# Sums of squares for the q and k norms as two rounded parts, with the gated-DeltaNet stages moved one or two k-tiles on

## The reference

```python
def l2norm(x):
    return x * lax.rsqrt(jnp.sum(x * x, axis=-1, keepdims=True) + EPS)
...
qkv, new_buf = causal_conv(jnp.concatenate([qg, kg, vg], axis=-1), conv_buf, conv_w)
q = l2norm(qkv[..., :GDN_KEY_W].reshape(B, L, GDN_HEADS, GDN_HEAD_DIM)) * (GDN_HEAD_DIM ** -0.5)
k = l2norm(qkv[..., GDN_KEY_W:2 * GDN_KEY_W].reshape(B, L, GDN_HEADS, GDN_HEAD_DIM))
v = qkv[..., 2 * GDN_KEY_W:].reshape(B, L, GDN_HEADS, GDN_HEAD_DIM)
```

## Time and profile before

| what | value |
| --- | --- |
| median of 3 runs | 3050.93 us (3047.31 to 3050.95) |
| the profiled execution's own time | 3054.05 us |
| its span, first to last instruction | 3052.3 us |
| PE busy | 2964.2 us, 22024 matmul records |
| DVE busy | 2036.2 us |
| ACT busy | 1203.9 us |
| POOL busy | 324.9 us |
| mean granted clock of TensorE | 0.990 of full speed |

### The profile page before, as it was taken

One profiled execution on the slowest core, in us unless ns is written; L12 is line 12 of the kernel. 1 busy time (PEld: TensorE's weight loads), 2 busy tenths in 40 slices (PEclk: granted clock), 3 DMA queues, 4 the chain that ended last, 5 costly groups with the idle time before them and its releaser, 6 DMA issues.

```text
span 3052.3 us, 52510 instructions
## 1 busy us (share of the span) xinstructions
PE 2964.2 (97%) x22024; PEld 2910.8 (95%) x22024; DVE 2036.2 (67%) x2828; ACT 1203.9 (39%) x1522; POOL 324.9 (11%) x433
## 2 busy tenths in 40 slices
PE   7999999999999999989999999999998999999998
PEld 7999999999999999988989999999997999999998
DVE  5556473747474656564567777777778878888885
ACT  4333333323333333332344444444444444444454
POOL 5010102011101010101210000000000000000111
PEclk9999999999999999999999999999999999999999
DMA  7233554523232334244334544445457666666665
GB/s 212 57 82 64 76 66 57 85 58 91 52 80 64 82 61 82 61 142 123 115 95 141 156 140 146 157 137 160 143 170 254 194 194 193 194 191 198 186 201 186
DMA packets 514107, 392.61 MB, mean 129 GB/s; under 512 B 16752, under 2 KB 483904, under 8 KB 513872
## 3 DMA queue, kind: packets, MB, share of 16 engines
q1 hardware_dynamic: 462272, 268.86, 35.9%
q0 software_dynamic: 22832, 88.39, 7.9%
q10 hardware_dynamic: 28768, 32.00, 3.6%
HBM read 304.87 MB, written 84.33 MB: 128 GB/s over the span
## 4 chain that ended last, share of the span: by engine, by line
PE 88%; DVE 7%; ACT 2%; issue 2%; DMA 1%; POOL 0%; DVEq 0%; SPq 0%; POOLq 0%; ACTq 0%
PE main L1268 39%; PE main L921 30%; PE mx L1268 6%; PE mx L1164 2%; PE mx L997 1%; PE mx L1065 1%; PE mx L1073 1%; PE mx L981 1%; DVE w_lo L1806 1%; DVE tmp L1914 1%; PE mx L1107 1%; ACT w_hi L1356 0%; PE mx L1171 0%; PE mx L1101 0%; PE mx L1045 0%
## 5 line engine op out<-in xcount | busy, mean ns | idle before, releaser
L921 PE MATMUL main<-h_hi,w_hi 128*128 128x296 f32 (+1 forms) x2592 | 612.1, 317 | 15.1 <-DVE h_lo L2164 8.4
L1268 PE MATMUL main<-forms_a,w_hi 128*128 128x288 f32 x3072 | 618.0, 297 | 8.7 <-DVE forms_a L2395 4.7
L1268 PE MATMUL main<-forms_b,w_hi 128*128 128x288 f32 x3072 | 613.9, 295 | 8.8 <-DVE forms_b L2395 5.0
L921 PE MATMUL main<-h_lo,w_hi 128*128 128x296 f32 (+1 forms) x2592 | 566.5, 300 | 0.0
L921 PE MATMUL main<-h_hi,w_lo 128*128 128x296 f32 (+1 forms) x2592 | 565.9, 300 | 0.0
L1268 PEld LDWEIGHTS main<-forms_a,w_hi 128*128 128x128 f32 x3072 | 497.1, 189 | 9.5 <-issue 9.3
L1268 PEld LDWEIGHTS main<-forms_b,w_hi 128*128 128x128 f32 x3072 | 492.1, 188 | 10.1 <-issue 5.6
L1268 PE MATMUL main<-forms_a,w_lo 128*128 128x288 f32 x1536 | 456.3, 297 | 0.0
L1268 PE MATMUL main<-forms_b,w_lo 128*128 128x288 f32 x1536 | 452.2, 294 | 0.0
L921 PEld LDWEIGHTS main<-h_hi,w_hi 128*128 128x128 f32 x2592 | 416.3, 191 | 27.2 <-DVE h_lo L2164 8.6
L921 PEld LDWEIGHTS main<-h_lo,w_hi 128*128 128x128 f32 x2592 | 423.7, 190 | 0.0
(11 more groups left out here) (383 smaller groups left out, 3685.0 us busy)
## 6 DMA issues: line engine op xcount, KB each, us to landing
w_raw<-in_w_in SPq DMA_DIRECT2D x130, 512.0 KB, 8.2
w_raw<-in_w_up SPq DMA_DIRECT2D x128, 512.0 KB, 4.1
w_raw<-in_w_down SPq DMA_DIRECT2D x100, 512.0 KB, 4.5
u_forms<-ub POOLq DMA_DIRECT2D x32, 1152.0 KB, 6.8
z<-x_scratch SPq DMA_DIRECT2D x32, 576.0 KB, 7.5
x_scratch<-z POOLq DMA_DIRECT2D x31, 576.0 KB, 3.1
stage<-u_forms ACTq DMA_DIRECT2D x30, 576.0 KB, 4.0
w_raw<-in_w_out SPq DMA_DIRECT2D x32, 512.0 KB, 4.0
```

What stands on the lines that cost most here:

```text
L921: ins = mm(out[:, half, :], w[:, ring, k, :], x[:, kx, half * width:half * width + width], start=first and n == 0, stop=last_ and n == 2)
L1268: ins = mm(out, w[:, k, :], x[:, kx, :], start=i in (0, 1, 3) and k == 0 and n == 0, stop=k == KP - 1 and n == 2, skip_group_check=True)
```

## The change

The squares are split as the projections' operands are. ACT writes a rounded copy `sq_hi` of the squares, DVE the rest `sq_lo` (in place of the squares), and PE multiplies both by a matrix of ones in `fp32r`: eight matmuls of one record each for four of two. Four GDN stages move by one or two positions, and all that come after them, but the last, by one: `norms` 14 to 16, `rows` 15 to 17, `scores` 20 to 21, `turn_v` 21 to 22, `turn_k` 22 to 23, `ws0` 23 to 24, `turn_r0` 24 to 25; the 32 stages from `t1` on filled 25 to 57 with one position free, and now fill 26 to 57 with none.

```diff
-GDN_STAGES = {"gates": 0, "norms": 14, "rows": 15, "scores": 20, "turn_v": 21, "turn_k": 22, "ws0": 23, "turn_r0": 24,
+GDN_STAGES = {"gates": 0, "norms": 16, "rows": 17, "scores": 21, "turn_v": 22, "turn_k": 23, "ws0": 24, "turn_r0": 25,
               **spread(["t1"] + T_STEPS + ["p64", "tp64", "vn0", "st0"]
-                       + [f"{s}_{c}" for c in range(1, NW) for s in ("ws", "vn", "st")], 25, 57),
+                       + [f"{s}_{c}" for c in range(1, NW) for s in ("ws", "vn", "st")], 26, 57),
...
+        sq_hi, sq_lo = (sq_mem[:, o:o + 2 * N].rearrange("p (a b) -> p a b", a=2) for o in (2 * 3 * CW + 5 * N, 2 * 3 * CW + 3 * N))
...
-                    token_sums(0, rs[:, 0, :])
-                    gpe.done(token_sums(2, rs[:, 1, :]), "norms")
+                    W(gdve, "sq_lo")
+                    for i in range(2):
+                        for half in range(2):
+                            cols = slice(half * HALF, half * HALF + HALF)
+                            mm(mx[:, 2 * i + half, 0:HALF], ones_r[:, :], sq_hi[:, i, cols], start=True, stop=False)
+                            ins = mm(mx[:, 2 * i + half, 0:HALF], ones_r[:, :], sq_lo[:, i, cols], start=False, stop=True)
+                    gpe.done(ins, "norms")
...
+                A(ones_r[:, :], ones[:, :], ACT.Copy)
...
                     done(A(rs, qkv[:, 0:2, :], ACT.Square), "square")
+                    W(gact, "square")
+                    done(A(sq_hi, rs, ACT.Copy), "sq_hi")
...
                 elif stage == "norms":
+                    W(gact, "sq_hi")
+                    done(TT(sq_lo, rs, sq_hi.bitcast(F32), ALU.subtract), "sq_lo")
                     W(gact, "rexp")
```

More of the change, by code:

```diff
@@ L197 @@
           + ["out"])
-GDN_ACT = (["conv_out", "exp", "ln", "sig", "zexp", "zln", "zsig", "square", "rln", "rexp", "brow", "eb", "decay",
+GDN_ACT = (["conv_out", "exp", "ln", "sig", "zexp", "zln", "zsig", "square", "sq_hi", "rln", "rexp", "brow", "eb", "decay",
             "vt", "r0", "t1"] + [f"{s}{b}" for b in INV[:-1] for s in ("p", "t")] + ["p64", "vn0", "o0"]
            + [f"{s}_{c}" for c in range(1, NW) for s in ("vn", "o")] + ["osq", "oln", "oexp"])
-GDN_DVE = (["conv_in", "conv_0", "conv_1", "conv_2", "last", "sel", "clamp", "zclamp", "qkv", "zs", "qn", "kn", "kb",
+GDN_DVE = (["conv_in", "conv_0", "conv_1", "conv_2", "last", "sel", "clamp", "zclamp", "qkv", "zs", "sq_lo", "qn", "kn", "kb",
             "vb", "diff", "keb", "qe", "dm", "at", "qkd", "tt0", "tt1", "kd", "r0"] + [f"t{b}" for b in INV[:-1]]
@@ L265, in hymba_kernel @@
         with ExitStack() as s:
+            sq_mem = sb("sq_mem", [P, 12200], F32R, stack=s)
+        with ExitStack() as s:
             tmp = sb("tmp", [P, 12200], stack=s)
@@ L290, in hymba_kernel @@
             one_hot = sb("one_hot", [16, 16], stack=s)
+            ones_r = sb("ones_r", [P, P], F32R, stack=s)
             dt_bias = sb("dt_bias_c", [16, 1], stack=s)
```

## The result

| | before | with the change |
| --- | --- | --- |
| median | 3049.67 us (3047.31 to 3050.95, 4 runs) | 3118.85 us (3113.84 to 3122.85, 4 runs) |
| ratio | | 1.0227, 95% interval 1.0215 to 1.0239 |
| span of the profiled execution | 3052.3 us | 3121.1 us |
| mean granted clock | 0.990 | 0.975 |

The change makes the kernel 69 us slower. The prediction said 3090, with a range of 3073 to 3106: the direction was right, the loss was 1.8 times the forecast of 39.

What follows compares the result with a forecast made beforehand. PE's nearly pauseless instruction list (busy 97%) was taken as the bound. Order 33.0, matmul saving included, plus clock 6 made 39 on the profiled 3054.05, or 3093; that execution lying 3.1 above the median, 3090 us, range 3073 to 3106.

Steps and rivals of the forecast that it cites:

- The order of the instructions: ACT's and DVE's order makes PE wait in each head: 4.13 us lost per head, 33.0 over eight, matmul saving included.
- the first stall: PE idles ahead of slot 10's first main matmul, waiting for DVE's weights: 2.66 us a head.
- the second: PE idles ahead of the norms, waiting for DVE's `sq_lo` behind an evacuation and a block of weights: 2.30 us a head.
- the move's own share: Part of the wait for slot 10's weights that the moved stages cause without the rounded copy: 1.43 us of 2.66.
- The third term: PE's wait ahead of the rows, for ACT's logarithm: 1.00 us a head in place of 0.78.
- The matmuls: Norms: eight `fp32r` records of 0.136, 1.09 us, replace eight of 0.235: 0.78 saved per head, 6.3 over eight.
- The stages behind: Stages after the rows (scores, `ws0`, slot 14) don't wait anew: together nothing, give or take 2 us.
- The clock: Every head loses full clock at least once; one half-speed stretch felt per head, 8 x 1.5 = 12, 6 more than now.
- The third rival: The clock stays down: two half-clock stretches per head fall on work, 33 + 18 = 51, 3102 us; chance 0.18.
- Only the matmuls count: ACT and DVE have both parts and slot 10's weights ready: gain 6.3, 3045, or 3039 if clock holds; chance 0.03.
- One stall only: Wait for slot 10's weights is real, but `sq_lo` is ready before PE reaches the norms: 3066 us; chance 0.08.
- the format does nothing: The norms' `fp32r` sums cost what the plain ones do: 33 + 6.3 + 6 = 45, 3096 us; chance 0.05.

Runs made afterwards that it cites:

- filled and padded kernel: Changed kernel with unread matmuls in place of PE's two stalls and the rows' matmuls on 128 partitions in place of 16: 3077.24 us, ratio 1.0097.
- padded kernel: Changed kernel with the rows' matmuls on 128 partitions, all but 16 holding zeros, in place of 16; both stalls stay: 3092.26 us, ratio 1.0140.
- rearranged program: Changed kernel with slot 10's weights made before the square, square, copy and rest before gate z is finished, rows at 18: 3037.93 us, ratio 0.9966.

## Why the prediction was wrong

**The order of the instructions: right.** By starts the first stall is 2.78 for 2.66, the second 2.29 for 2.30, the move's own share 1.54 for 1.43, with both releasers as named. The third term, a wait of 1.00 ahead of the rows in the place of 0.78, was not: in the filled and padded kernel it is 0.79 by starts, and in the changed kernel 0.15. The filled and padded kernel puts the price of the order at 32 us (4.0 a head) for the forecast 33.0.

**The matmuls: right.** Eight records in 1.15 us at full clock, for 1.09. In the changed kernel itself nothing of it arrives, as the norms run at half speed in 2.11.

**The stages behind: nearly right.** I had 2 us either way. A wait of 0.53 is new in each head: one of PE's transpositions in the inverse stands behind DVE's step `t32`, which now comes after slot 13's weights.

```profile
344.57 0.66 PE L1002 MATMUL mx<-ident,tmp 128*128 128x128 f32 x4 [0.54 <-DVE tmp L1997]
```

The prediction looked at the boundaries of slots 11 and 14 and not at this one. The wait of 0.91 of the earlier trace rows fell to 0.53 in exchange. That leaves 0.15 a head, about 1 us in all, inside the 2 us allowed.

**The clock: the step that failed.** The prediction says: "If one such stretch falls on work that PE can't hide in a stall, it is 8 x 1.5 = 12, 6 more than now; if two, 18 more; none at all, 6 less. I take 6, because slow k-tiles between two stalls only shorten the stalls." It took one short fall in each head as felt, 12 us in all less the 6 that the kernel before already pays. Measured is 44 us (5.5 a head) less the 5 that the kernel before pays (four falls of 1.3), so 39 in the place of 6. With 32 for the order that makes 71, beside 69 measured. The price of a stretch was about right, their number was not: four stretches end to end in every head, 4 x 1.5 = 6.0 by the prediction's own price, for 5.5 measured. The third rival, "the clock stays down", named the mechanism but stopped at two stretches, 3102, and so the range ended at 3106.

Two things were overlooked. The prediction expected slow k-tiles between the two stalls, where they would only shorten the second one. But the k-tile there ran at full speed; the clock fell at 294.4, late in the second stall, and took the norms, the k-tile behind, the rows and about three more k-tiles, which PE can't hide, so ACT's logarithm, too, started late. And the rows were counted at their length of full clock, though the kernel before shows that a wait of 0.61 and rows of 2.15 are enough to lose the clock in four of eight heads. At half clock the same rows are 4.22 long. The padded kernel shows what they do there: 6.8 us of half speed for 13.6, and 27 us off the time, for rows that do the same sums on more partitions. That it is their doubled length that keeps the clock down is likely but not shown by itself.

The Trainium skill (TensorE: Matmul & The Clock Gate, What's actually happening) has the clock set by recent activity. The runs agree: the fillers, 34 useless matmuls a head, made the changed kernel 27 us faster.

**Rivals.** "Only the matmuls count" was the other side, given 0.03. It took a rearranged program to get there, at 3038, near the 3039 that the rival named with the clock holding. "One stall only" fell with the two stalls in the profile, and "the format does nothing" with the eight records in 1.15 us.

## What to carry to other kernels

Before a stage is moved by a few positions, read where it lands in every engine's own order: a position on PE's list that crosses a boundary of slots can put whole blocks of other work ahead of the stage on the engines that feed it. Where PE is the bound, price a stall twice, once as idle time and once as the clock that the work behind it loses, and count that work at its half-speed length. If a step grows on ACT or DVE, first look for work in the same slot that nobody waits for and put the step ahead of it.

## What the runs showed of the hardware

- Plain float32 matmuls from 16 partitions and from 128 are as long (0.407 and 0.412 us a record), but behind the former the granted clock fell to half in four of eight heads and behind the latter in none. The wait of 0.61 ahead was the same.
- Two stalls of 2.5 and 2.1 us with one k-tile between them took the clock to half speed in every head of the padded kernel, for 6.8 us, at a cost of 2.1.
- A fall of the clock costs about 1.3 us when it meets plain work once, and 5.5 when two stalls and the 16-partition matmuls follow each other. That is more than the two causes cost one by one (1.7 and 2.1).
- In four of the profiled executions PE paused once in a run of small matmuls, for 1.0 to 5.7 us, with no releaser in the profile; with three of the four the clock fell to half. Its cause stays open; this is the longest:

```profile
625.68 0.27 PE L1075 MATMUL mx<-tmp 128*128 128x64 f32 x1 [5.65 <-issue]
```
